# Even mixer: the score matmuls of two pairs of heads at one place in TensorE's order

## The chip, the cores and the metric

The kernel runs on one core of a Trainium2 chip. The metric is the device time of one execution in microseconds, the median of the runs. It is one program of 25,386 instructions that computes a whole small model once, so there is no loop over launches; what counts is the time from the first instruction to the last.

## The reference

Two stacks of two layers each on 256 positions of width 1024. The change touches only the even mixer of the second stack, which has eight forgetting heads (a) and four differential heads (b), each of the latter with two softmax maps:

```python
def forgetting_attention(q, k, v, cum_logf):
    ...
        s = jnp.einsum('bqhd,bkhd->bhqk', q[:, qs:qe], k[:, :qe], ...) * scale
        s = s + cum_logf[:, :, qs:qe, None] - cum_logf[:, :, None, :qe]
        p = jax.nn.softmax(jnp.where(causal, s, -jnp.inf), axis=-1).astype(v.dtype)
        outs.append(jnp.einsum('bhqk,bkhd->bqhd', p, v[:, :qe]))

def differential_attention(q, k, v, lam):
    ...
        s = jnp.einsum('bqhjd,bkhjd->bhjqk', q[:, qs:qe], k[:, :qe], ...) * scale
        p = jax.nn.softmax(jnp.where(allowed, s, -jnp.inf), axis=-1)
        p = (p[:, :, 0] - lam * p[:, :, 1]).astype(v.dtype)
        outs.append(jnp.einsum('bhqk,bkhe->bqhe', p, v[:, :qe]))

def even_mixer(h, w_in, ...):
    a_q, a_k, a_v, a_f, b_q, b_k, b_v = split_cols(h @ w_in, EVEN_SIZES)
    ...                     # norms, rotation, forgetting_attention, differential_attention
    b_out = (rms_norm(b_out, subln_gain) * (1.0 - lambda_init)).reshape(bsz, seq, B_WIDTH)
    return jnp.concatenate([a_out, b_out], axis=-1) @ w_out
```

Queries come in blocks of 128 (`Q_BLOCK`), so a head's scores are a 128x128 and a 128x256 block. `HEAD_DIM` is 64.

## The kernel before

**Weights.** All weights stream through one pipeline of units of 128x1024 elements: SyncE loads a unit into `RAW` (4 buffers), ScalarE rounds it to `WH` (L1332), VectorE subtracts to `WL` (L1620; 5 buffers each). Each K-tile of a projection of 512 columns then takes, for each of the two blocks of 128 rows, three matmuls into a PSUM bank `M` (L1057 to L1059). The conversion of unit u+4 stands in the order where unit u begins.

**The order.** A planner, `Plan`, gives each step a place `at`; one unit of place is one K-tile of 512 columns for both row blocks (six matmuls). `Plan.order` sorts the steps once for TensorE (and GpSimd) by `at`, and once each for ScalarE and VectorE by `at + late + LATER[kind]`. Each engine issues its steps strictly in that order. The places of the steps off the weight stream are numbers written by hand in the table `PLACES`, relative to the end of a projection. A step on the second of a pair's maps or heads has `late` added on ScalarE and VectorE, but not on TensorE.

**The banks.** Everything off the weight stream shares four PSUM banks `AUX`. The planner gives each step the bank that is due to be free first:

```python
        for s in steps:
            ...
            if s.kind in BANKED:
                b = min(range(4), key=lambda b: busy[b])
                use[b] += 1
                s.bank, s.use = b, use[b]
                busy[b] = s.at + s.late + HELD.get(s.kind, 1.5)
```

On the chip TensorE waits at such a step until the bank's former content is used up (`aux_out`), and every later matmul waits with it. `HELD` is 3.0 for `df_s` and 3.5 for `hg_s`.

**One head's steps.** `df_s` (differential, two maps j = 0, 1) and `hg_s` (forgetting, or the odd mixer's; two heads hh = 0, 1): a pair of scores; its matmuls use 64 of the 128 rows of TensorE's array each, issued alternately for the two members (L1219 to L1222), at the place of the second member. VectorE adds the mask and takes the row maximum (L1889, L1890), ScalarE the exponential with its row sum (L1537, L1538), which frees the bank. `df_p` (L1900 to L1910) or `hg_p` (L1916 to L1921): VectorE scales. `pt`: three transposes on TensorE (L1229), copied by ScalarE (L1559). `df_o`: output matmuls (L1240 to L1242) into a bank that ScalarE empties (L1567 to L1573); `hg_o` the output of two pairs (L1256, L1258).

**The order around the change.** With the mixer's start as place 0, the projections end at bq 8, af 10, bk 18, bv 26, aq 34, ak 42, av 50, then the memory keys kx00 58 and kx01 66, and the output projection at 82. Score places: differential 30.1, 34.2, 39.5, 44.5 (heads 0 to 3, from bv's end); forgetting 51.3, 56.6, 61.6, 66.3 (pairs 0 to 3, from av's end). In between on ScalarE and VectorE lie the projections' evictions with squares (`hq`, L1375, L1379; sums L1831), the reciprocal roots (`rsq`, L1385, L1388), the scalings `hn` (L1790), and the exchange transposes `bt` (L1738). The norm of the differential output (`bo_v`, `bo_n`) is followed by two groups of transposes (`turn`, L1101) at 60.4 and 62.7.

Of the kernel before, what the change touches and what calls it, by code (L numbers as in the profile page):

```python
# [32 lines left out]
    "df_late": (1.5, 0.6, -0.6, -0.1), "df_p": (3.1, 3.4, 3.4, 3.4), "df_pt": (5.9, 6.8, 6.2, 6.8), "df_o": (7.4, 9, 10.5, 8.3),  # L33
    "bo": (28, 28.5, 29.2, 30.1, 34.4, 36.7), "hg_s": (1.3, 6.6, 11.6, 16.3), "hg_late": (1.3, 1.3, 1.9, 2.5),
    "hg_p": (3, 5.4, 4.2, 5.4, 4.2, 5.4, 4.2, 6.6), "hg_pt": (5.6, 6.8, 5.6, 6.2, 5, 7.4, 6.5, 7.4), "hg_o": (7.6, 8.2),
    "od_s": (0.9, 6, 9.8, 15.5), "od_late": (0, 1.3, -1.2, 1.3), "od_p": (3, 5.4, 4.2, 4.2, 1.7, 5.4, 4.8, 6),
    "od_pt": (5.6, 9.3, 5.3, 7.5, 5.3, 6.5, 6.5, 7.7), "od_o": (9.6, 11.9), "odd": (25.7, 17.5, 0, 14.2, 0, 14.8, -7.2),
# [2319 lines left out]
```

## Time and profile before

| | |
|---|---|
| median of 3 runs | 1866.26 us (1866.19 to 1866.61) |
| the profiled execution | 1867.07 us, of which the span 1865.2 us |
| busy, of the span | TensorE 1859.0, weight loads 1623.3, VectorE 1310.1, ScalarE 1122.3, GpSimd 370.0 us |
| granted TensorE clock | 1.000 (mean) |
| DMA | 233 GB/s from and to HBM over the span |

The span runs from the first to the last instruction. An engine's busy time is the time in which it executes something; matmuls overlap in the record, so the distance between the starts of two matmuls says what one costs, not its duration. In a timeline the bracket at the end is the idle time ahead of the instruction and what ended it.

### The profile page before, as it was taken

What the parts mean: (1) busy time and instruction counts of PE and PEld (TensorE: products, weight loads), DVE (VectorE), ACT (ScalarE), POOL (GpSimd) and SP (SyncE); (2) the same over time, 40 slices, a digit from 0 to 9 for tenths busy, and PEclk for the clock granted to TensorE, in tenths of its full rate; (3) what the DMA queues carried; (4) which work ended last, traced back from release to release, by engine and by line L of the source; (5) the groups of instructions that cost most, each with busy time, mean ns of one, the idle gap of its engine ahead of it and who ended that gap; (6) DMA issues with size and microseconds to landing.
All of it is one profiled execution on the core that took longest, in us unless ns stands there. A gap on an engine that the chain in (4) does not pass through costs nothing.

```text
span 1865.2 us, 25386 instructions
## 1 busy us (share of the span) xinstructions
PE 1859.0 (100%) x9283; PEld 1623.3 (87%) x9283; DVE 1310.1 (70%) x1945; ACT 1122.3 (60%) x1678; POOL 370.0 (20%) x606
## 2 busy tenths in 40 slices
PE   9999999999999999999999999999999999999999
PEld 7888988888889888888888889888888888899888
DVE  6776776667777776666577886776666578877664
ACT  6776655557766655555468785654555467766552
POOL 2101223111001441122103001531122111102220
PEclk9999999999999999999999999999999999999999
DMA  9767789878578998798765567997788787758884
GB/s 315 236 189 221 223 261 302 257 233 254 165 214 245 287 283 238 217 274 256 237 181 189 174 193 203 278 277 239 225 253 255 223 277 231 215 158 235 252 257 136
DMA packets 289659, 436.43 MB, mean 234 GB/s; under 512 B 25532, under 2 KB 170144, under 8 KB 289280
## 3 DMA queue, kind: packets, MB, share of 16 engines
q1 hardware_dynamic: 260240, 352.41, 61.8%
q0 software_dynamic: 28832, 82.07, 16.1%
q8 instruction: 74, 1.21, 0.3%
q14 instruction: 49, 0.40, 0.1%
q10 hardware_dynamic: 464, 0.34, 0.1%
HBM read 396.43 MB, written 38.29 MB: 233 GB/s over the span
## 4 chain that ended last, share of the span: by engine, by line
PE 97%; DVE 2%; DMA 1%; issue 0%; SPq 0%; ACT 0%; POOL 0%; DVEq 0%; POOLq 0%; ACTq 0%
PE M L1057 31%; PE M L1058 30%; PE M L1059 30%; PE AUX L1101 1%; DVE WL L1620 0%; DMA SQI<-squares 0%; PE AUX L1115 0%; DMA RAW<-in_w_in 0%; PE AUX L1229 0%; PE AUX L1221 0%; DMA squares<-SQO 0%; PE AUX L1219 0%; DVE DS L1939 0%; PE AUX L1272 0%; PE AUX L1301 0%
## 5 line engine op out<-in xcount | busy, mean ns | idle before, releaser
L1620 DVE TENSOR_TENSOR WL<-RAW,WH 128x1024 fp32r<-128x1024 f32 (+1 forms) x670 | 811.2, 1216 | 380.5 <-ACT WH L1332 378.1
L1332 ACT ACTIVATE WH<-RAW 128x1024 fp32r<-128x1024 f32 (+1 forms) x670 | 706.3, 1056 | 518.5 <-PE M L1059 466.8
L1057 PE MATMUL M<-WH,Bh 128*128 128x512 f32 (+1 forms) x1820 | 691.5, 380 | 0.6 <-DVE Bl L1647 0.6
L1059 PE MATMUL M<-WH,Bl 128*128 128x512 f32 (+1 forms) x1820 | 683.1, 375 | 0.0
L1058 PE MATMUL M<-WL,Bh 128*128 128x512 f32 (+1 forms) x1820 | 683.1, 375 | 0.0
L1057 PEld LDWEIGHTS M<-WH,Bh 128*128 128x128 f32 x1820 | 344.2, 189 | 50.3 <-issue 4.2
L1059 PEld LDWEIGHTS M<-WH,Bl 128*128 128x128 f32 x1820 | 344.2, 189 | 47.2
L1058 PEld LDWEIGHTS M<-WL,Bh 128*128 128x128 f32 x1820 | 344.4, 189 | 44.8
L1370 ACT ACTIVATE AS<-M,KEEP 128x256 f32<-128x256 f32 x132 | 55.4, 471 | 75.6 <-PE M L1059 74.1
L1057 PE MATMUL M<-WH,MTh 128*128 128x512 f32 x128 | 51.0, 398 | 0.0
L1058 PE MATMUL M<-WL,MTh 128*128 128x512 f32 x128 | 48.5, 379 | 0.0
L1059 PE MATMUL M<-WH,MTl 128*128 128x512 f32 x128 | 48.5, 379 | 0.0
L2045 POOL DMA_DIRECT2D squares<-QT x4 | 3.1, 763 | 176.1 <-DVE QT L1738 176.1
L2058 POOL DMA_DIRECT2D HB1t<-squares x48 | 26.5, 558 | 53.2 <-DMA squares<-HB1b 47.1
L2058 POOL DMA_DIRECT2D HB0t<-squares x48 | 26.4, 557 | 50.0 <-DMA squares<-HB0b 45.7
L2058 POOL DMA_DIRECT2D HD0t<-squares x48 | 26.5, 559 | 45.1 <-DMA squares<-HD0b 36.1
L2038 POOL TENSOR_TENSOR KEEP<-SM,KEEP 128x2 f32<-128x2 f32 x15 | 13.4, 896 | 110.0 <-DVE SM L1696 100.5
L1711 DVE SCALAR_TENSOR_TENSOR X<-M,X 128x512 f32<-128x512 f32 (+1 forms) x54 | 30.5, 607 | 6.4 <-PE M L1059 6.4
L2058 POOL DMA_DIRECT2D HC0t<-squares x48 | 26.4, 556 | 42.2 <-DMA squares<-HC0b 41.3
L2058 POOL DMA_DIRECT2D HC1t<-squares x48 | 26.4, 556 | 40.1 <-DMA squares<-HC1b 40.1
L1467 ACT ACTIVATE JK<-X 128x512 f32<-128x512 f32 x52 | 32.8, 630 | 1.3 <-DVE X L1711 0.2
L1057 PE MATMUL M<-WH,FA0h 128*128 128x512 f32 x88 | 33.4, 379 | 0.0
(533 smaller groups left out, 2894.9 us busy)
## 6 DMA issues: line engine op xcount, KB each, us to landing
RAW<-in_ffn_w_in SPq DMA_DIRECT2D x352, 256.0 KB, 4.1
RAW<-in_w_in SPq DMA_DIRECT2D x103, 512.0 KB, 4.7
RAW<-in_w_gate_up SPq DMA_DIRECT2D x176, 256.0 KB, 4.5
RAW<-in_ffn_w_out SPq DMA_DIRECT2D x88, 512.0 KB, 4.6
RAW<-in_w_down SPq DMA_DIRECT2D x44, 512.0 KB, 5.4
RAW<-in_x_w_kv SPq DMA_DIRECT2D x32, 512.0 KB, 4.4
RAW<-in_even_w_in SPq DMA_DIRECT2D x24, 512.0 KB, 4.5
RAW<-in_odd_w_in SPq DMA_DIRECT2D x24, 512.0 KB, 5.1
```

Of the source, the lines that this page charges most:

```text
L1057: e.matmul(out, s.hi, wh, start=s.at0, stop=False)
L1058: e.matmul(out, s.hi, wl, start=False, stop=False)
L1059: i = e.matmul(out, s.lo, wh, start=False, stop=s.final)
L1101: tr = e.transpose(aux[:, i * P:(i + 1) * P], x, ident)
L1332: e.activation(p.WH[:, h, 0:s.size], p.RAW[:, i, 0:s.size], ACT.Copy).then_inc(k.w_hi, 1)
L1370: e.activation(s.silu[t], banks[t][:, 0, :], ACT.Silu, scale=r[t]).then_inc(k.silu_made, 1)
L1467: e.activation(p.JK, s.srcs[t], ACT.Square, accum_out=s.ss[:, 2 * t + s.half:2 * t + s.half + 1]).then_inc(k.sq_sum, 1)
L1620: e.tensor_tensor(p.WL[:, h, 0:s.size], p.RAW[:, s.u % NRAW, 0:s.size], hi.bitcast(F32), ALU.subtract).then_inc(k.w_lo, 1)
L1711: e.scalar_tensor_tensor(out=x, in0=banks[t], scalar=s.scale, in1=x, op0=ALU.mult, op1=ALU.add).then_inc(k.m_out[c.banks[t]], 1)
L2038: e.tensor_tensor(s.r, s.v, p.MHALF, ALU.pow).then_inc(k.r_made, 1)
L2045: e.dma_start(p.parked[x.slot, 0:4 * P * 32 * x.m].rearrange("(c p e) -> p c e", c=n, p=P), x.squares.rearrange("p (c e) -> p c e", c=n)). ...
L2058: e.dma_start(x.rows[32 * c:32 * c + 32, :].rearrange("p (q e) -> p q e", q=q), p.parked[x.slot, c * n:(c + 1) * n].rearrange("(q j e) -> ...
```

## The change

Six places and four lags of the table `PLACES` change; no operation is added or removed. In `df_s` the scores of differential head 1 get the place of head 0, and those of head 3 the place of head 2. In `hg_s` the first forgetting pair gets the place of the second, and the third that of the fourth. All later steps of a head or pair are placed relative to its scores and move with them, but for the two `hg_o`, which hang on the second and fourth pair. `hg_late` gives each pair 0 or 0.6 in place of 1.3, 1.3, 1.9 and 2.5. Eight matmuls of one pair and eight of the next then follow each other in TensorE's order.

```diff
-    "kx10": (5.7, 7.6, 11.4, 26), "kx11": (6.7, 8.8, 15.5, 27.5), "cu": (1, 2, 8, 8.5, 18, 1.5, 31), "df_s": (4.1, 8.2, 13.5, 18.5),
+    "kx10": (5.7, 7.6, 11.4, 26), "kx11": (6.7, 8.8, 15.5, 27.5), "cu": (1, 2, 8, 8.5, 18, 1.5, 31), "df_s": (4.1, 4.1, 13.5, 13.5),
     "df_late": (1.5, 0.6, -0.6, -0.1), "df_p": (3.1, 3.4, 3.4, 3.4), "df_pt": (5.9, 6.8, 6.2, 6.8), "df_o": (7.4, 9, 10.5, 8.3),
-    "bo": (28, 28.5, 29.2, 30.1, 34.4, 36.7), "hg_s": (1.3, 6.6, 11.6, 16.3), "hg_late": (1.3, 1.3, 1.9, 2.5),
+    "bo": (28, 28.5, 29.2, 30.1, 34.4, 36.7), "hg_s": (6.6, 6.6, 16.3, 16.3), "hg_late": (0, 0.6, 0, 0.6),
     "hg_p": (3, 5.4, 4.2, 5.4, 4.2, 5.4, 4.2, 6.6), "hg_pt": (5.6, 6.8, 5.6, 6.2, 5, 7.4, 6.5, 7.4), "hg_o": (7.6, 8.2),
```

Where the steps concerned stand before and after, in TensorE's order, with the bank that the rule above gives them:

| step | place before | place after | bank after, and whose content it held |
|---|---|---|---|
| scores of head 1 (`df_s`) | 34.2 | 30.1 | 2, 0: transposed keys |
| scaling, transposes, output of head 1 | 37.6, 41.0, 43.2 | 33.5, 36.9, 39.1 | output: 3, head 0's second map |
| scores of heads 2 and 3 (`df_s`) | 39.5, 44.5 | 39.5, 39.5 | 1, 2 and 0, 3: transposes 0, 1, outputs 0, 1 |
| scaling, transposes, output of head 3 | 47.9, 51.3, 52.8 | 42.9, 46.3, 47.8 | transposes: 0, head 3's first map |
| scores of pairs 0 and 1 (`hg_s`) | 51.3, 56.6 | 56.6, 56.6 | 1, 3 and 0, 2 |
| first `turn` of the differential output | 60.4 | 60.4 | 0: first head of pair 1 (head 2) |
| transposes of heads 0 and 1 | 56.9, 58.1 | 62.2, 63.4 | |
| scores of pairs 2 and 3 (`hg_s`) | 61.6, 66.3 | 66.3, 66.3 | 0, 2 and 1, 3 |
| transposes of heads 4 and 5 | 66.6, 69.0 | 71.3, 73.7 | |

## Rows read from the trace of the kernel before

**Rows 1.** The page, busy time, share of the span and instructions of each engine.

```profile
PE 1859.0 (100%) x9283; PEld 1623.3 (87%) x9283; DVE 1310.1 (70%) x1945; ACT 1122.3 (60%) x1678; POOL 370.0 (20%) x606
```

**Rows 2.** The waits of TensorE: line, releaser, us in total, times, longest us.

```profile
PE M L1010 <- DVE WARM L1595: 1.1, 1, 1.1
...
PE M L1032 <- ACT Bh L1393: 0.5, 1, 0.5
```

**Rows 3.** Timeline of TensorE around one score group: start us, us, instruction.

```profile
985.19 0.38 PE L1059 MATMUL M<-WH,Bl 128*128 128x512 f32 x1
...
985.83 0.38 PE L1059 MATMUL M<-WH,Bl 128*128 128x512 f32 x1
986.14 0.37 PE L1219 MATMUL AUX<-KB,QB 64*128 64x128 f32 x1
...
986.69 0.38 PE L1221 MATMUL AUX<-KB,QB 64*128 64x256 f32 x1
...
987.32 0.38 PE L1058 MATMUL M<-WL,Bh 128*128 128x512 f32 x1
```

**Rows 4.** Timeline of TensorE, single steps: the opening, then the differential heads.

```profile
1.06 3.81 PE L1010 MATMUL M<-WARM 128*128 128x256 bf16 x19 [1.06 <-DVE WARM L1595]
...
995.28 0.49 PE L1229 MATMUL AUX<-CC,TMP 128*128 128x128 f32 x3
...
1000.90 0.37 PE L1219 MATMUL AUX<-KB,QB 64*128 64x128 f32 x1
...
1011.04 0.60 PE L1115 MATMUL AUX<-CC,TMP 128*128 128x128 f32 x4
```

**Rows 5.** Timeline of ScalarE, differential heads and the first memory keys.

```profile
989.30 1.06 ACT L1332 ACTIVATE WH<-RAW 128x1024 fp32r<-128x1024 f32 x1 [1.63 <-PE M L1059]
990.27 0.35 ACT L1537 ACTIVATE TMP<-AUX,SM 128x128 f32<-128x128 f32 x1
...
991.07 0.37 ACT L1537 ACTIVATE TMP<-AUX,SM 128x128 f32<-128x128 f32 x1
...
995.54 1.06 ACT L1332 ACTIVATE WH<-RAW 128x1024 fp32r<-128x1024 f32 x1
996.50 0.47 ACT L1559 ACTIVATE TMP<-AUX 128x384 f32<-128x384 f32 x1
...
1000.09 0.35 ACT L1567 ACTIVATE BO<-AUX,SM 128x128 f32<-128x128 f32 x1
...
1001.28 0.23 ACT L1385 ACTIVATE SM<-SM 128x16 f32<-128x16 f32 x1
...
1013.42 0.22 ACT L1385 ACTIVATE SM<-SM 128x16 f32<-128x16 f32 x1 [1.05 <-DVE SM L1833]
...
1034.28 1.06 ACT L1332 ACTIVATE WH<-RAW 128x1024 fp32r<-128x1024 f32 x1 [0.86 <-PE M L1059]
...
1035.62 0.68 ACT L1375 ACTIVATE TMP<-M,KEEP 128x512 f32<-128x512 f32 x1
...
1038.11 0.35 ACT L1537 ACTIVATE TMP<-AUX,SM 128x128 f32<-128x128 f32 x1
```

**Rows 6.** Timeline of VectorE, differential heads and the last forgetting heads.

```profile
1001.90 0.30 DVE L1889 CUSTOM_DVE_ANT_0 AUX<-AUX,C 128x128 f32<-128x128 f32 x1 [2.04 <-PE AUX L1222]
...
1002.50 1.22 DVE L1620 TENSOR_TENSOR WL<-RAW,WH 128x1024 fp32r<-128x1024 f32 x1
...
1009.60 0.22 DVE L1900 RECIPROCAL SM<-SM 128x2 f32<-128x2 f32 x2
...
1010.77 1.22 DVE L1620 TENSOR_TENSOR WL<-RAW,WH 128x1024 fp32r<-128x1024 f32 x1
1011.91 1.27 DVE L1831 TENSOR_REDUCE SM<-AS 128x8 f32<-128x512 f32 x2
...
1056.20 0.16 DVE L1916 RECIPROCAL SM<-SM 128x2 f32<-128x2 f32 x1
...
1056.87 1.30 DVE L1738 STREAM_TRANSPOSE QB<-TMP 128x512 f32<-128x512 f32 x2
```

## The prediction

> **What bounds the kernel now.** The page comes first: TensorE is busy 1859.0 of 1865.2 us, VectorE 70%, ScalarE 60% [rows 1]. The list of waits agrees: over the span TensorE waits four times for others, 2.9 us in all, 1.1 the longest (first and last of the four in [rows 2]). So every microsecond of issue saved on TensorE shortens the program, and every wait put into its queue lengthens it. The two other engines have slack only as long as what they owe TensorE is ready at its place.
>
> Next, TensorE's timeline around one score group [rows 3]. A K-tile for one row block (three matmuls, half a unit of place) costs 985.83 - 985.19 = 0.65 us, 0.216 a matmul. The last weight matmul starts at 985.83, the second after the group at 987.32: 1.49 us for what takes 0.43 without the group, so a group costs 1.06 us. Eight half-height matmuls run two by two; the last two passes step 0.216 (256 columns), the others by half, so the work itself is 2 x 0.108 + 2 x 0.216 = 0.65. The other 0.41 is lost around the group: 0.09 before it, 0.11 in its first step, the rest on the way back.
>
> **What the change removes.** Eight score groups become four. If the second pair of a group pays its 0.65 alone, each merge saves 0.41, and four save 1.64 us. Bounds: 0 (the second pair pays as much) to 1.64; I take 1.64, since its tile shape is that of the pair before it. The Trainium skill, "TensorEngine Tiling (Array Packing)", Key Properties, says that a change of tiling mode drains TensorE; with the 166 ns constant that "TensorE: Matmul & The Clock Gate", Single matmul latency, gives, two drains a group make an estimated 0.33 instead of 0.41, and the four merges 1.33 instead of 1.64. The sum goes by the row's 0.41.
>
> **What it moves: differential heads.** Places are relative to the mixer's start; one unit is 1.29 us of weight matmuls. Head 1 goes from 34.2 to 30.1 with its scaling (33.5), transposes (36.9) and output (39.1), head 3 from 44.5 to 39.5 (42.9, 46.3, 47.8). The cover that this takes is ScalarE's. I follow the queues with the durations of before. On TensorE three transposes are three steps of 0.11 and one output six (0.67), at no switch.
>
> (a) Transposes of head 0, place 36.0. ScalarE sorts the exponentials by place + late + 2.0, so head 0's second map (late 1.5) is now the fourth of four instead of the second of two. The conversion ahead of them starts when TensorE reaches place 32: 989.30 [rows 5], now 0.65 later. 989.95 + 0.97 + 4 x 0.80 = 994.12; the scaling on VectorE, 1.17 (1009.60 to 1010.77 [rows 6]) and a tail of 0.1, ends at 995.4. TensorE comes at 995.28 - 0.41 = 994.87 [rows 4]. Wait 0.55.
>
> (b) Output of head 0, 37.5. It wants the copied transposes; ahead of the copy on ScalarE stand a conversion (0.97), the query eviction and squares (2.49, from 1035.62 to 1038.11) and another conversion (0.96, 995.54 to 996.50): 994.12 + 4.43 = 998.55, and 0.47 until the copy has landed [rows 5]: 999.02. TensorE is there at 995.4 + 2 x 0.33 + 3 x 0.65 = 998.0. Wait 1.0.
>
> (c) Scores of heads 2 and 3, 39.5. The least-busy rule gives them the banks of transposes 0 and 1, output 0 and output 1. Output 1 stands directly ahead (39.1, nothing between). TensorE issues it (0.67) and the pair of head 2 (0.85), then wants output 1's bank, which ScalarE begins to empty 0.85 after that output started and for 1.19 (1000.09 to 1001.28 [rows 5]) and a tail of 0.1: 2.14 - 1.52 = 0.6.
>
> (d) Output of head 3, 47.8. Before, VectorE worked without a gap from 1001.90 [rows 6] until the query reduction for which ScalarE waited 1.05 us (1013.42 [rows 5]). Now its first reduction starts at 1004.0: the scores of 39.5 stood at 1000.90 [rows 4], less 0.41, plus transposes 0.33 and output 0.67 moved ahead, plus 1.5 of waits is 1003.0, plus 0.85 of issue and 0.17 to land. Into the same stretch come two more reductions (0.60 each, 1001.90 to 1002.50) and head 3's scaling (1.17): ScalarE's reciprocal root moves from 1013.42 to 1013.42 + 2.1 + 2.4 = 1017.9. In order behind it: root 0.37, copy 0.37, conversion 0.97, copy of head 3, 0.47: 1020.1. TensorE: 1011.04 [rows 4] + 2.15 of waits - 0.82 of merges = 1012.4, then 0.44 + 6 x 0.65 + 2 x 0.33 and about 0.3 of short waits at 44.6, 45.7 and 46.3 (the projection's transposes and the two scalings, just late): 1017.7. Wait 2.4, with rounding 2.5.
>
> Differential half: 0.55 + 1.0 + 0.6 + 0.3 + 2.5 = 4.95, less 0.82 = +4.1.
>
> **Forgetting heads.** Heads 0 and 1 go from 51.3 to 56.6, 4 and 5 from 61.6 to 66.3; their transposes become 62.2, 63.4, 71.3 and 73.7. TensorE is not short of work meanwhile: weights fill it.
>
> (e) First transposes of the differential output, 60.4. Before, that bank had been emptied of transposes. Now all four banks hold scores. Three have the same due time, the rule takes the lowest number, and that is head 2's first map, third in ScalarE's order. ScalarE, from TensorE's place 58 (1034.28 before [rows 5]): 0.15 + conversion 0.97 + eviction and squares 2.49 + three exponentials 2.4 + 0.1 = 6.1. TensorE needs 5 x 0.65 = 3.2 from 58 to 60.4. Wait 2.9.
>
> (f) At 62.8, scalings of heads 1 and 3 come behind a conversion: 0.2. At 71.3 VectorE owes four reductions (2.4), one over squares (1.27 and 0.1), a conversion (1.14, 1010.77 to 1011.91), a block transpose (1.3) and a scaling (0.67, 1056.20 to 1056.87 [rows 6]), 6.9; it starts 1.8 after the group's first matmul, a conversion being in hand: 8.7. TensorE is there after 0.2 + 2 x 0.65 + 10 x 0.65 = 8.0, and 0.1 for the way back: 0.6. The later output at 74.5 waits 0.05.
>
> Forgetting half: 2.9 + 0.2 + 0.6 + 0.05 = 3.75, less 0.82 = +2.9.
>
> **Costed at nothing.** The number of operations on ScalarE, VectorE and GpSimd is the same, and no DMA is added. Conversions fall back by up to 4 us, but each is issued eight units (10.4 us) before its weights are used; without that cover each would stop TensorE itself.
>
> **The sum.** 8.7 us of waits less 1.64 is +7.0. The profiled execution took 1867.07 (span 1865.2 and 1.9 around it): 1874.1. It stands 0.8 above the median of the runs, so 1873.3.
>
> **Rivals.**
> *Waits absorbed.* ScalarE was idle at many places before: 1.63 ahead of the conversion at 989.30, 1.05 at 1013.42 [rows 5]. If these took up the bunching, the merge gain alone is left: -1.64, 1864.6, within 0.2%. Against it: in (a), (b) and (e) that idle is a wait for TensorE's place, which does not move earlier. It decides from the point at which the waits sum to under 5.4 us (1.64 + 3.7); (d) and (e) alone are 5.4.
> *The clock falls behind a wait.* No wait before is longer than 1.1 us, these are up to 2.9, and no row shows such a gap amid full work. At the start the 256-column matmuls take 0.20 each (19 in 3.81 us, the first of [rows 4]) against 0.216 for 512 later, so the lower of the two levels (1.2 against 2.4 GHz). As long a stretch at that rate after (d) and (e) would cost 1.9 us each: 1877.1. The Trainium skill, "TensorE: Matmul & The Clock Gate", Why this matters for your kernels, warns of clock loss after idle gaps between bursts; no row here shows it in mid-run.
> *Weights late.* If conversions slip beyond 10.4 us because reloads wait for them too, TensorE waits at L1057. None of the four waits of before is for converted weights, and the reserve is more than twice the slip. Half the slip uncovered would add 2 us: 1875.3.
>
> **How the numbers follow.** Measurement tells 0.2%, 3.7 us, from no change. Forecast 0.81, absorbed 0.10, clock 0.05, weights 0.03, and 0.01 for a gain above 3.7, for which no term is large enough. Sizes: with ScalarE's and VectorE's durations all 5% shorter the same sum is +4.9, all 5% longer +8.9; a merge worth nothing adds 1.6. The low end reaches towards the absorbed case, to 1870.0; the high end is 1876.0. Faster 0.01, within 0.2% 0.10, slower 0.89.
>
> **What would show it.** Four groups of sixteen half-height matmuls, each 1.71 us from weight matmul to weight matmul. TensorE's waits: at the score line (L1219) 0.6 on ScalarE's output eviction; at L1240 for ScalarE's copy, 1.0 and 2.5; at L1101 2.9 for an exponential. Granted clock 1.00 throughout. I am wrong if the waits at (d) or (e) are missing: then the queue ahead of them was shorter than counted, or another bank was given.

## The result, and the profile after

| | before | after |
|---|---|---|
| median of 6 runs each | 1866.59 us (1866.19 to 1868.76) | 1874.45 us (1873.73 to 1879.52) |
| ratio | | 1.0046, 95% interval 1.0036 to 1.0056 |
| the profiled execution, span | 1867.07, 1865.2 | 1876.93, 1875.1 |

The change makes the kernel 0.46% slower. (The ratios here and below are those on record; they are not exactly the quotients of the medians, which here is 1.0042.) Of the numbers in `PLACES` it moves four places (not six), two in `df_s` and two in `hg_s`, and four lags. The six runs fall into two kinds. Three have a mean granted clock of 1.000 and lie within 1873.73 to 1874.14, 7.2 us above before. Three have 0.999 or 0.997 and lie at 1874.75, 1876.93 and 1879.52. The profiled execution is one of the latter, so two things have to be read from its trace: the waits, and what the clock did.

The page's busy line and the list of TensorE's waits (line, releaser, us in total, times, longest), which answer to [rows 1, 2]:

```profile
PE 1861.1 (99%) x9283; PEld 1625.0 (87%) x9283; DVE 1309.9 (70%) x1945; ACT 1120.1 (60%) x1678; POOL 368.0 (20%) x606
```

```profile
PE AUX L1101 <- ACT TMP L1538: 3.0, 1, 3.0
PE AUX L1240 <- ACT TMP L1559: 2.2, 1, 2.2
...
PE AUX L1240 <- issue: 0.7, 1, 0.7
...
PE AUX L1219 <- ACT JK L1573: 0.6, 1, 0.6
PE AUX L1229 <- DVE TMP L1910: 0.5, 1, 0.5
```

Instruction counts are as before, and the busy time of every engine is within 2.4 us of it. Five waits are new in this mixer, and 1.1 us is no longer the longest. Every one stands at a step that the forecast names: (a) at L1229, (b) and (d) at L1240, (c) at L1219, (e) at L1101.

The same in TensorE's timeline, which answers to [rows 3, 4]:

```profile
987.11 0.38 PE L1059 MATMUL M<-WH,Bl 128*128 128x512 f32 x1
987.42 0.37 PE L1219 MATMUL AUX<-KB,QB 64*128 64x128 f32 x1
...
989.25 0.38 PE L1058 MATMUL M<-WL,Bh 128*128 128x512 f32 x1
...
996.81 0.55 PE L1229 MATMUL AUX<-CC,TMP 128*128 128x128 f32 x3 [0.49 <-DVE TMP L1910]
...
1000.36 0.46 PE L1240 MATMUL AUX<-VB,TMP 128*128 128x128 f32 x2 [0.73 <-issue]
...
1006.03 0.34 PE L1219 MATMUL AUX<-KB,QB 64*128 64x128 f32 x1 [0.65 <-ACT JK L1573]
...
1021.64 0.69 PE L1240 MATMUL AUX<-VB,TMP 128*128 128x128 f32 x2 [2.24 <-ACT TMP L1559]
...
1047.07 0.63 PE L1101 MATMUL AUX<-CC,BO 128*128 128x128 f32 x4 [2.96 <-ACT TMP L1538]
```

A merged group costs 989.25 - 987.11 - 0.43 = 1.71 us. Two single ones would be 2.12, so a merge saves 0.41. A bracket says how long TensorE stood idle. What a wait adds to the program is a little more. The bracket opens only where the last matmul ends, 0.38 us after its start, while the next would have started 0.22 after it; and the first step behind the wait is longer (0.33, from 1021.67 to 1022.00 in the last trace below, where without a wait it is 0.22). Measured from start to start, like a group, the five add 0.71, 0.97, 0.92, 2.5 and 3.15 us.

What the forecast did not put into its sum stands in the windows behind wait (d): busy time and number of PE, PEld, DVE, ACT, POOL, then TensorE's granted clock, the DMA share and GB/s. Below them the matmuls of that stretch.

```profile
1020.00:1022.00 2.00, 0.36 (x2) 0.36 (x3) 1.90 (x6) 2.00 (x4) 0.00 (x0) 0.95 0.55 201
1022.00:1024.00 2.00, 2.00 (x9) 1.82 (x9) 2.00 (x3) 1.31 (x5) 0.00 (x0) 0.50 0.66 225
1024.00:1026.00 2.00, 2.00 (x11) 1.68 (x10) 0.61 (x1) 1.19 (x4) 0.00 (x0) 0.70 0.58 178
1026.00:1028.00 2.00, 2.00 (x15) 1.79 (x14) 0.00 (x0) 1.20 (x3) 0.00 (x0) 1.00 0.80 298
...
1046.00:1048.00 2.00, 0.93 (x7) 0.91 (x8) 1.93 (x7) 2.00 (x11) 0.00 (x0) 1.00 0.65 246
1048.00:1050.00 2.00, 2.00 (x11) 1.76 (x10) 1.43 (x3) 1.43 (x3) 0.00 (x0) 1.00 0.00 0
```

```profile
1023.40 0.63 PE L1058 MATMUL M<-WL,Bh 128*128 128x512 f32 x1
1023.83 0.63 PE L1059 MATMUL M<-WH,Bl 128*128 128x512 f32 x1
```

After the wait the clock stands at its lower level (0.50, or 1.2 of 2.4 GHz) for 3.4 us, and a matmul steps 0.43 us instead of 0.216. Against the same steps at full clock, the stretch from 1021.64 until the clock is back loses some 1.7 us. Behind the longer wait (e), in the same execution, the clock stays at 1.00.

### The profile page after: what moved, and what is told of

It reads as the page before. It is cut to its first block, busy times and chain, and to the rows that moved or that the text cites. A ratio compares the mean times of both kernels' runs of the same rounds, so it can differ in the third digit from the quotient of the medians.

```text
span 1875.1 us, 25385 instructions
## 1 busy us (share of the span) xinstructions
PE 1861.1 (99%) x9283; PEld 1625.0 (87%) x9283; DVE 1309.9 (70%) x1945; ACT 1120.1 (60%) x1678; POOL 368.0 (20%) x606
## 4 chain that ended last, share of the span: by engine, by line
PE 93%; DVE 3%; DMA 1%; ACT 1%; issue 1%; SPq 0%; POOL 0%; ACTq 0%; DVEq 0%; POOLq 0%
PE M L1057 29%; PE M L1058 29%; PE M L1059 29%; DVE WL L1620 1%; DMA RAW<-in_w_in 1%; PE AUX L1101 1%; ACT WH L1332 0%; DMA SQI<-squares 0%; PE AUX L1115 0%; PE AUX L1229 0%; DMA squares<-SQO 0%; PE AUX L1221 0%; DVE DS L1939 0%; PE AUX L1272 0%; DVE SM L1831 0%
## 5 line engine op out<-in xcount | busy, mean ns | idle before, releaser
L1057 PEld LDWEIGHTS M<-WH,Bh 128*128 128x128 f32 x1820 | 344.5, 189 | 49.8 <-issue 3.6
L2058 POOL DMA_DIRECT2D HB0t<-squares x48 | 26.3, 555 | 48.8 <-DMA squares<-HB0b 44.5
```

The costliest lines, as they stand in the source:

```text
L1057: e.matmul(out, s.hi, wh, start=s.at0, stop=False)
L2058: e.dma_start(x.rows[32 * c:32 * c + 32, :].rearrange("p (q e) -> p q e", q=q), p.parked[x.slot, c * n:(c + 1) * n].rearrange("(q j e) -> ...
```

## The experiments

Each was timed against the kernel before on the same chip. "Full-clock runs" are those whose mean granted clock is shown as 1.000. Kernels that differ by a number of `PLACES` are given by that number.

**The differential half alone.**

```diff
-"df_s": (4.1, 8.2, 13.5, 18.5),
+"df_s": (4.1, 4.1, 13.5, 13.5),
```

> Only the differential heads' places are changed; the forgetting pairs stand as before. Queue theory (waits of TensorE for steps that have come late in ScalarE's and VectorE's order): two merged groups of 1.71 us, waits at L1229 0.5, L1240 1.0 and 2.3, L1219 0.65 to 0.9, no wait at L1101; +4.1 us on before, and the granted clock falls in some executions, then +1 to +2 more. Rival, that the loss is mostly one bank's assignment at the first transposes of the differential output: +1 at most.

Measured: 1872.4 us (8 runs), before 1866.64, ratio 1.0027 (1.0017 to 1.0038). Its three full-clock runs have a median of 1871.34, +4.7 where +4.1 was expected; five are at 0.999 and lie at 1872.4 to 1873.0. Its waits:

```profile
PE AUX L1240 <- ACT TMP L1559: 2.2, 1, 2.2
...
PE AUX L1219 <- ACT JK L1573: 0.7, 1, 0.7
PE AUX L1240 <- issue: 0.6, 1, 0.6
PE AUX L1229 <- DVE TMP L1910: 0.6, 1, 0.6
```

Waits (a) to (d) are here and (e) is not: they belong to the differential heads.

**The forgetting half alone.**

```diff
-"hg_s": (1.3, 6.6, 11.6, 16.3), "hg_late": (1.3, 1.3, 1.9, 2.5),
+"hg_s": (6.6, 6.6, 16.3, 16.3), "hg_late": (0, 0.6, 0, 0.6),
```

> Only the forgetting pairs' places and lags are changed; the differential heads stand as before. Queue theory: two merged groups, a wait at L1101 of 1.3 and one at L1229 of up to 1.8 behind it, together 3.0 to 4.5; +2.3 to +2.9 us on before; no loss of clock, as no wait is above 2.2. With the first half alone at +4.1 the two halves then add up to the whole, 7.0. Rival (a pool of slack that both halves drain, so that the halves are not additive): each half alone under +2.

Measured: 1869.16 us (10 runs, all at full clock), ratio 1.0014 (1.0005 to 1.0023): +2.5. Waits:

```profile
PE AUX L1229 <- DVE TMP L1921: 1.5, 1, 1.5
...
PE AUX L1101 <- ACT TMP L1538: 1.4, 1, 1.4
```

Without the earlier banks of the differential half, the wait of the mixer's second half splits: 1.4 for an exponential, 1.5 for a scaling. In full-clock runs the halves add up, 4.7 + 2.5 = 7.2, which is the change.

**The change with the first `turn` later**, at 62.9 instead of 60.4, so that it no longer asks for a bank while four pairs of scores hold all of them.

```diff
-"bo": (28, 28.5, 29.2, 30.1, 34.4, 36.7),
+"bo": (28, 28.5, 29.2, 30.1, 36.9, 36.7),
```

> The change whole, but the first transposes of the differential output stand at place 62.9 instead of 60.4, so that the 3.0 us wait for the third exponential's bank is not met at 60.4. Queue theory: ScalarE's queue is what is late, so the wait comes back at the transposes of the forgetting heads at 62.2 and 62.8 (0.3, 0.9 and 1.7 by the queues worked through): about the same time as the change, within 0.7 us of it. Rival, that the bank given by the least-busy rule is the cause by itself: 2.9 us faster than the change.

Measured: 1873.85 us (4 runs), ratio 1.0040 (1.0026 to 1.0054); three full-clock runs at 1873.06, 1873.33 and 1874.36. TensorE's timeline:

```profile
1043.84 0.52 PE L1229 MATMUL AUX<-CC,TMP 128*128 128x128 f32 x3 [0.37 <-ACT TMP L1538]
1044.96 0.55 PE L1229 MATMUL AUX<-CC,TMP 128*128 128x128 f32 x3 [0.61 <-DVE TMP L1921]
1048.07 0.55 PE L1229 MATMUL AUX<-CC,TMP 128*128 128x128 f32 x3 [1.48 <-DVE TMP L1921]
```

The wait at L1101 is gone, and 0.37 + 0.61 + 1.48 = 2.46 us of its 2.95 are back at the forgetting heads' own transposes. The bank mostly decided which instruction waited: the full-clock median is 0.5 us under that of the change, not 2.9. What is late is the softmax of four maps standing together, and whoever needs it first pays.

**All four merges kept, and the places behind them set anew** from the queues of the trace. The scores of heads 0 and 1 go a little earlier (29.3), the forgetting pairs 0 and 1 one unit later; the lags sort ScalarE's and VectorE's work so that each map is ready in the order of its transposes, and the outputs of heads 1 and 3 and the `turn` stand later.

```diff
-"df_s": (4.1, 4.1, 13.5, 13.5), "df_late": (1.5, 0.6, -0.6, -0.1), "df_o": (7.4, 9, 10.5, 8.3),
+"df_s": (3.3, 3.3, 13.5, 13.5), "df_late": (-2.1, -0.2, -0.1, -0.1), "df_o": (7.4, 13.4, 10.5, 9.3),
-"bo": (..., 34.4, 36.7), "hg_s": (6.6, 6.6, 16.3, 16.3), "hg_late": (0, 0.6, 0, 0.6),
+"bo": (..., 38.4, 37.2), "hg_s": (7.6, 7.6, 16.3, 16.3), "hg_late": (-0.8, 0.6, 0.0, 2.9),
-"hg_p": (3, 5.4, 4.2, 5.4, 4.2, 5.4, 4.2, 6.6), "hg_pt": (5.6, 6.8, 5.6, 6.2, 5, 7.4, 6.5, 7.4), "hg_o": (7.6, 8.2),
+"hg_p": (3, 4.4, 4.2, 4.3, 3.1, 4.6, 4.2, 4.6), "hg_pt": (5.4, 6.8, 5.6, 6.8, 5.0, 7.4, 6.5, 7.4), "hg_o": (7.4, 8.7),
```

> All four merges kept, and the steps behind them given later or reordered places and lags (df_o, df_late, the two transposes of the differential output, hg_p, hg_pt, hg_late, and the first group of forgetting pairs one unit later), chosen so that by the queues worked through no step of TensorE waits over 0.1 us. Queue theory: no wait in the list beyond those of before, four groups of 1.71, clock 1.00, 1.5 us faster than before (1865.1). Rival, that packing the scores costs time by itself (ScalarE's and VectorE's load in a burst): 2 us or more slower than before whatever the places.

Measured: 1865.25 us (11 runs, all at full clock), before 1866.64, ratio 0.9994 (0.9985 to 1.0003). Of the waits above 0.25 us none is left in this mixer; what the list shows is from other places, the first from the opening:

```profile
PE M L1010 <- DVE WARM L1595: 1.1, 1, 1.1
PE M L1057 <- DVE Bl L1647: 0.5, 2, 0.3
PE M L1032 <- ACT Bh L1393: 0.4, 1, 0.4
PE M L1032 <- DVE WL L1620: 0.3, 1, 0.3
```

The same kernel once more:

> The kernel with all four merged groups and the places behind them set anew, once more, beside the kernel before on the same chip: 1865.2, that is 1.3 us or 0.07% under the kernel before. Queue theory: the only difference that remains is the four saved switches, 1.64 us less 0.2 to 0.4 of waits that remain. Rival, the merged groups save nothing: 1866.5, no difference.

Measured: 1865.82 us (11 runs), before 1866.57, ratio 0.9996 (0.9987 to 1.0005). Each interval holds 1. Put together, the 22 runs have a median of 1865.5, and 20 of them lie below 1866.64, the median of the 71 runs of the kernel before that stood beside the experiments; none of those 71 lies below 1865.5. So this version is some 1.1 us (0.06%) under both kernels, far below the 0.2% that counts here as a difference. The traces show it where the change is: from a step ahead of the mixer's scores (L1101, at 943.63 in the trace of before) to a later one that moved in neither kernel (L1115, at 1093.74) are 150.11 us before and 149.06 in both profiled executions of this version, 1.05 less.

**The same places with the merges undone:** the second pair of each group stands half a unit behind the first, and every other step where it was (the numbers of the second pairs that count from their scores are half a unit smaller).

```diff
-"df_s": (3.3, 3.3, 13.5, 13.5), ... "hg_s": (7.6, 7.6, 16.3, 16.3),
+"df_s": (3.3, 3.8, 13.5, 14.0), ... "hg_s": (7.6, 8.1, 16.3, 16.8),
```

> The kernel with the places behind the scores set anew, but with the second pair of each scores step half a unit after the first, so that TensorE does them in eight groups instead of four; every other step stands at the same place as there. If a merged group saves one switch of TensorE's tiling (0.41 us each, 1.64 in all), this is 1.64 us slower than the merged one: 1866.7 to 1867.3 against 1865.25, so within 0.1% above the kernel before. Rival, the gain over the kernel before came from the new places and not from the merging: the same time as the merged one, 1865.2.

Measured: 1867.93 us (11 runs, all at full clock), beside the 1865.82 above on the same chip: 2.1 us apart, and 0.6 above the range that was expected. The new places are not what gained: without the merges they cost 1.09 us between the same two steps (151.20), with them they save 1.05. TensorE's timeline around the split group, and the one wait that the split kernel has in this mixer:

```profile
986.70 0.38 PE L1059 MATMUL M<-WH,Bl 128*128 128x512 f32 x1
987.01 0.37 PE L1219 MATMUL AUX<-KB,QB 64*128 64x128 f32 x1
...
988.19 0.38 PE L1058 MATMUL M<-WL,Bh 128*128 128x512 f32 x1
```

```profile
PE AUX L1240 <- ACT TMP L1559: 0.5, 1, 0.5
```

A single group costs 988.19 - 986.70 - 0.43 = 1.06 as before; eight of them are 8.48 us against 4 x 1.71 = 6.84, so 1.64 of the 2.1. The wait, which adds 0.5 from start to start and had not been expected, is the rest.

**The change with the output of head 3 later**, at 49.8 instead of 47.8: wait (d) mostly away, wait (e) left.

```diff
-"df_o": (7.4, 9, 10.5, 8.3),
+"df_o": (7.4, 9, 10.5, 10.3),
```

> The change, with one place moved: the output of differential head 3 stands at 49.8 instead of 47.8. In the trace of the changed kernel TensorE waited 2.2 us there for that head's copied transposes, and in some executions its clock then stood at half for some 3 us. Queue theory: the wait shrinks to about 0.9 us, the 3.0 us wait at the first transposes of the differential output (L1101) stays; +5.4 us on the kernel before, 1872.0. If the clock falls only behind that wait amid the shorter ones ahead of it, all runs are at a clock of 1.000 and none is above 1872.5. Rival, the clock falls for a reason that has nothing to do with that wait: some of the runs again show 0.999 and lie 1 to 2 us above the others. Rival, the time of the chain is fixed by the softmax work of ScalarE and the wait only moves to the next step: 1873.7 as the changed kernel.

Measured: 1872.89 us (4 runs), ratio 1.0035 (1.0021 to 1.0048). The one full-clock run is 1871.60, +5.0, or 2.2 less than the change in such runs; in the waits 2.24 is gone and 0.66 has come at L1115, 1.6 less. The clock did not do what was expected: three of four runs are at 0.999. In the profiled one it fell behind (e):

```profile
1040.00:1042.00 2.00, 0.00 (x0) 0.00 (x0) 1.59 (x5) 2.00 (x11) 0.00 (x0) 1.00 0.43 161
1042.00:1044.00 2.00, 1.90 (x7) 1.75 (x8) 1.36 (x6) 2.00 (x6) 0.00 (x0) 0.54 0.26 101
1044.00:1046.00 2.00, 2.00 (x8) 1.59 (x7) 1.96 (x5) 0.19 (x1) 0.00 (x0) 0.61 0.00 0
```

So the fall does not belong to wait (d) alone.

**One wait by itself.** The kernel with the places set anew, its `df_o` of head 3 pulled ahead from 9.3 to 7.4.

> The kernel with the places set anew, and the output of differential head 3 pulled ahead to 46.9 from 48.8: one single wait of about 3 us for that head's copied transposes, with no other wait in the 30 us ahead of it. Queue theory: 3.0 us of wait less 0.2 that it absorbs behind it, 1868.0. If a wait of this size alone lowers the clock, as in some executions of the change, some of the runs show a clock of 0.999 and lie at 1869.5 to 1870. If it takes the shorter waits ahead of it as well, all runs are at 1.000 and within 1867.7 to 1868.4.

Measured: 1870.01 us (10 runs), ratio 1.0021 (1.0012 to 1.0031); eight runs at 0.999 or 0.998, nine over 1869.3. The lowest, 1868.38, is where the queues alone put it. TensorE's wait and the windows behind it:

```profile
1016.60 0.49 PE L1240 MATMUL AUX<-VB,TMP 128*128 128x128 f32 x2 [2.95 <-ACT TMP L1559]
```

```profile
1016.00:1018.00 2.00, 1.41 (x9) 1.35 (x10) 2.00 (x3) 0.97 (x4) 0.00 (x0) 1.00 0.62 201
1018.00:1020.00 2.00, 2.00 (x6) 1.61 (x5) 0.43 (x1) 1.28 (x6) 0.00 (x0) 0.50 0.31 102
```

With no other wait ahead of it, one wait of 2.95 us is enough for a fall; it takes no row of shorter ones. The lower level begins 1.4 us after TensorE has resumed.

**A wait of 2.3 and one of 1.65 us**, the same output at 8.0 and at 8.4. (The first expectation counts nine runs of the last kernel as fallen; by the clock as shown it is eight.)

> The kernel with the places set anew, with the output of differential head 3 at 47.5 (46.9 gave one wait of 2.95 us, and nine of ten executions then had a clock of 0.999 or 0.998). The single wait should be about 2.2 us. If the length of the wait makes the fall likely, fewer executions fall than nine in ten, as with the 2.2 us wait of the change: the median lies at 1867.4 without falls and 1869 with them. Rival: any single wait of over 2 us does it as surely as 3 us, nearly all executions are at 0.999 and the median is 1869.

> The same with the output of differential head 3 at 47.9: a single wait of about 1.7 us. The kernel with only the forgetting half changed had waits of 1.5 and 1.7 us and its clock fell in none of ten executions; so all executions at 1.000 and 1866.9. Rival: a single wait of 1.7 us amid full work does lower the clock in some executions, and they lie 1.5 to 2 us higher.

Measured, at 8.0: 1869.62 us (10 runs), before 1866.84, ratio 1.0012 (1.0003 to 1.0022). Four full-clock runs within 1867.49 to 1867.83, six at 0.999 within 1869.39 to 1871.76. Six of ten against eight of ten at 2.95 us are too few runs to say that the longer wait makes the fall likelier. At 8.4: 1867.37 us (10 runs, 1866.87 to 1868.03), ratio 1.0003 (0.9994 to 1.0013), all at full clock. TensorE's timeline of each:

```profile
1017.64 0.50 PE L1240 MATMUL AUX<-VB,TMP 128*128 128x128 f32 x2 [2.30 <-ACT TMP L1559]
```

```profile
1017.00 0.49 PE L1240 MATMUL AUX<-VB,TMP 128*128 128x128 f32 x2 [1.65 <-ACT TMP L1559]
```

The kernel without the wait was not timed beside these two; it lies 1.1 us under the kernel before, which here makes 1865.7. Against that the shorter wait costs 1.6 us (1.74 in the trace, between the two steps named above). The longer one costs 2.0 while the clock holds, and 3.7 to 6.0 when it does not.

**The changed kernel once more.**

> The changed kernel once more, for the share of executions in which the clock falls: about half of them at 1.000 and within 1873.7 to 1874.2, the others at 0.999 or less and 1 to 5 us above; median 1874.5. If the falls of the first comparison were a matter of that chip, none here.

Measured: 1874.62 us (4 runs, 1873.15 to 1875.05), ratio 1.0040 (1.0025 to 1.0055); two runs at 0.999. The two kinds are not apart here as was expected: 1873.15 and 1874.65 at full clock, 1874.58 and 1875.05 at 0.999. This time the profiled execution (1874.65) is at full clock, with the same waits: the same program, the same idle time, another clock. TensorE around wait (d), the window behind it, and ScalarE:

```profile
1019.06 0.38 PE L1059 MATMUL M<-WH,Bl 128*128 128x512 f32 x1
1021.67 0.49 PE L1240 MATMUL AUX<-VB,TMP 128*128 128x128 f32 x2 [2.24 <-ACT TMP L1559]
...
1022.66 0.38 PE L1058 MATMUL M<-WL,Bh 128*128 128x512 f32 x1
```

```profile
1022.00:1024.00 2.00, 2.00 (x16) 1.82 (x15) 2.00 (x3) 1.92 (x8) 0.00 (x0) 1.00 0.71 239
```

```profile
999.84 0.47 ACT L1559 ACTIVATE TMP<-AUX 128x384 f32<-128x384 f32 x1
...
1019.46 0.22 ACT L1385 ACTIVATE SM<-SM 128x16 f32<-128x16 f32 x1 [2.29 <-DVE SM L1833]
...
1020.20 1.05 ACT L1332 ACTIVATE WH<-RAW 128x1024 fp32r<-128x1024 f32 x1
1021.14 0.48 ACT L1559 ACTIVATE TMP<-AUX 128x384 f32<-128x384 f32 x1
```

This is the trace for checking the sum. Wait (d), for example, from start to start: 1022.66 - 1019.06 = 3.60 us from the last weight matmul ahead of the output to the second behind it; an output without a wait takes 1.10 (997.34 to 998.44 in the trace of before), so the wait adds 2.50. From the first matmul of its first score group (987.47) to the last output of the forgetting heads (1070.81) are 83.34 us; before, they are 76.37. The difference is 6.97. In the first profile of the change the same distance is 85.01, and the 1.67 more is the stretch at half clock; the other 1.3 of the 9.9 us between the two spans arose ahead of the first score group, where the change touches nothing.

## Why the prediction was right

The predicted 1873.3 lies 1.15 us under the median of 1874.45, inside the range; in full-clock runs the change is +7.2 where +7.0 was worked out. The mechanism was right, and so was the sum but for one term, (f), whose excess happened to offset three that were too small: that part is luck. The sum put the clock at nothing, and it adds 0.6 us to the median. Step by step:

| step | predicted | measured, start to start |
|---|---|---|
| four merges | -1.64 | -1.64 (groups of 1.71; split again: +1.64 of 2.1) |
| (a) transposes of head 0 | 0.55 | 0.71 |
| (b) output of head 0 | 1.0 | 0.97 |
| (c) scores of heads 2 and 3 | 0.6 | 0.92 |
| short waits at 44.6 to 46.3 | 0.3 | 0.13 |
| (d) output of head 3 | 2.5 | 2.50 |
| (e) first `turn` | 2.9 | 3.15 |
| (f) 62.8, 71.3, 74.5 | 0.85 | 0.14 (at 74.5 alone) |
| sum | +7.0 | +6.9 |

**The merges.** The second pair of a group pays only its own matmuls, as its tile shape suggested. The Trainium skill, "TensorEngine Tiling (Array Packing)", Key Properties, says that only a change of mode drains the array; the rows agree (a group of two pairs costs 1.71, a single one 1.06 and the second pair's own matmuls 0.65). The estimate of 1.33 for four merges, which the prediction worked out with that page and the 166 ns of the Trainium skill, "TensorE: Matmul & The Clock Gate", Single matmul latency, was 0.3 too low.

**(a) to (c)** came from ScalarE's queue. The last trace shows how: four pairs of exponentials stand where two stood, and the copy that (b) needs starts at 999.84 and takes 0.47, the output starting at 1000.41. The list of waits calls this "issue" and not the copy; the order of times shows the copy. (c) is 0.3 too small because a wait costs more from start to start than the idle time that I counted.

**(d)** was a chain over three engines, and it held in its middle too. The reciprocal root was put at 1017.9 on the clock of the trace of before; it is at 1019.46, and that trace runs 987.47 - 986.14 = 1.33 later, so at 1018.1. The copy of head 3 was to end at 1020.1; on the same scale it starts at 1019.8 and takes 0.48, so it ends 0.2 later. ScalarE's idle time ahead of the root grew from 1.05 [rows 5] to 2.29: the slack on which the rival "waits absorbed" rests was itself a wait for VectorE's queue.

**(e)** had the right instruction, releaser and size. The experiment with the later `turn` limits what the bank means: it chose the place of the wait and little of its length.

**(f)** is the mis-sized term: 0.6 at 71.3 and 0.2 at 62.8 did not come. The waits are differences of two queues of some 8 us, and VectorE's was counted too long by one item that stood elsewhere. The last trace shows it, TensorE first, then VectorE:

```profile
1057.27 0.37 PE L1219 MATMUL AUX<-KA,QA 64*128 64x128 f32 x1
...
1065.36 0.49 PE L1229 MATMUL AUX<-CC,TMP 128*128 128x128 f32 x3
```

```profile
1059.03 0.29 DVE L1889 CUSTOM_DVE_ANT_0 AUX<-AUX,NB 128x128 f32<-128x128 f32 x1
...
1064.03 0.16 DVE L1916 RECIPROCAL SM<-SM 128x2 f32<-128x2 f32 x1
...
1065.34 1.30 DVE L1738 STREAM_TRANSPOSE QB<-TMP 128x512 f32<-128x512 f32 x2
```

TensorE comes 8.1 us after the group's first matmul, as counted. VectorE starts 1.76 after it (1.8 counted) and takes 5.00 for reductions and conversion (4.9 counted). Then the scaling comes at once, and the block transpose, counted 1.3 ahead of it, stands behind it. So the scaling is done 7.5 us after the first matmul and not 8.7, and nobody waits. This excess of 0.7 offset the 0.7 by which (a), (c) and (e) were too small.

**The rivals.** Waits were not absorbed. Weights were never late: no wait behind the score groups is for a converted unit. (The list of before holds five waits in its four lines, not four; none of them is for converted weights.) The clock did fall behind a wait, in 3 of 6 runs and 2 of 4. All runs of the first comparison above 1874.2 are such runs. I gave it 0.05 and thought of both long waits; it is rather a chance at each execution than a fixed cost. Its price of 1.9 us, read off the opening, was near the measured 1.7, though the opening shows the lower level only in its steps: the profile's granted clock reads 1.00 there. The Trainium skill, "TensorE: Matmul & The Clock Gate", Why this matters for your kernels, warns of a loss of clock after idle gaps between bursts. The runs agree that one gap amid full work can do it, but here 2.24 and 2.30 us were enough, which is shorter than the gaps that it warns of.

**Where the gain went.** The merges gave what they can (1.64), and the waits took 8.5: ScalarE and VectorE got the softmax of two pairs at once in front of steps that did not move. With the later steps placed by the new queues the waits vanish, and the merge gain alone is left, less a small rest: -1.1 us.

## What to carry to other kernels

Where one engine is full and the others are "only" 60 to 70% busy, moving two steps together is free on the full engine and not on the others: follow the queue of each helper to the next step that waits for it, and move those steps in the same edit. A saving of 0.41 us per tile switch is real but is lost to a single wait of that size; count both before merging. When runs of one program scatter by more than its neighbours' do, compare their granted clocks before explaining a difference.

## What the runs showed of the hardware that was not expected

A single wait in mid-run can halve TensorE's clock, and it does so only in some executions of the same program:

| longest wait in the mixer | kernels | runs with a clock under 1.000 |
|---|---|---|
| none to 0.5 us | places anew (twice), split | 0 of 33 |
| 1.5 and 1.65 us | forgetting half; output at 8.4 | 0 of 20 |
| 2.2 to 2.3 us | differential half; turn later; output at 8.0 | 12 of 22 |
| 2.95 us | output at 7.4; head 3's output later | 11 of 14 |
| 2.24 and 2.95 us | the change (twice) | 5 of 10 |

None of the 71 runs of the kernel before beside the experiments is under 1.000 either. Five of the profiled executions have a fall. In each of their traces the lower level begins after TensorE has resumed: 0.1 to 0.4 us after in the change, in the kernel with head 3's output later and in the one with 2.30 us, 1.2 in the differential half alone, 1.4 in the one with a single wait of 2.95. In each it lasts 3.4 us, which costs half of that, 1.7 us. By the runs of the kernel with 2.3 us of wait a fall costs 1.6 to 4.3 (1869.39 to 1871.76 against 1867.49 to 1867.83). A mean clock of 0.997, as in the execution of 1879.52, is a loss of some 5.6 us of 1878, more than one such fall; that execution was not profiled, and where its clock fell stays open. Why two long waits (5 of 10) do not lead to more falls than one (11 of 14) stays open too; the counts are small. Between 1.65 and 2.24 us nothing was tried.
